# Modulation sums on VectorE and row tiles modulated piece by piece in a two-layer attention block on one Trainium2 core

## The reference

```python
def hybrid_layer(x, ctx, c, c_ctx, lw, pos, update_ctx):
    mod_x = jax.nn.silu(c) @ lw['ada_w'] + lw['ada_b']          # ada_w is 1024 x 3072
    mod_c = jax.nn.silu(c_ctx) @ lw['ada_w'] + lw['ada_b']
    shift, scale, gate = jnp.split(mod_x[:, None, :], 3, axis=-1)
    c_shift, c_scale, c_gate = jnp.split(mod_c, 3, axis=-1)
    h = rmsnorm(x, lw['norm_w']) * (1 + scale) + shift
    hc = rmsnorm(ctx, lw['norm_w']) * (1 + c_scale) + c_shift
    p = h @ lw['w_in']
...
    x = x + gate * merge_branches(o_m, o_s, o_a, z_m, z_s, z_a, g, lw)
    if update_ctx:                                               # layer 0 only
...
        ctx = ctx + c_gate * merge_branches(oc_m, oc_s, oc_a, zc_m, zc_s, zc_a, gc, lw)
    return x, ctx

def merge_branches(o_m, o_s, o_a, z_m, z_s, z_a, g, lw):
...
    y = jax.nn.sigmoid(g_m) * y_m + jax.nn.sigmoid(g_s) * y_s + jax.nn.sigmoid(g_a) * y_a
    return y @ lw['w_out']
```

## Time and profile before

| what | value |
|---|---|
| median of three runs | 2024.87 us (2021.86 to 2031.04) |
| profiled execution, its own time | 2025.76 us |
| its span | 2024.0 us |
| TensorE busy, share of the span | 89% |
| VectorE, ScalarE, GpSimd | 52%, 53%, 30% |
| layer 0's merge stage | 925.82 to 1100.52 us |
| layer 0's output projection | 1100.52 to 1177.94 us |
| layer 1's merge stage | 1869.32 to 1964.22 us |

### The profile page before, as it was taken

One profiled execution on the slowest core, in us unless ns is written; L12 is line 12 of the kernel. 1 busy time (PEld: TensorE's weight loads), 2 busy tenths in 40 slices (PEclk: granted clock), 3 DMA queues, 4 the chain that ended last, 5 costly groups with the idle time before them and its releaser, 6 DMA issues. The chain is left out here.

```text
span 2024.0 us, 27323 instructions
## 1 busy us (share of the span) xinstructions
PE 1794.5 (89%) x10749; PEld 1547.1 (76%) x10749; DVE 1048.1 (52%) x2082; ACT 1075.1 (53%) x1933; POOL 599.1 (30%) x328
## 2 busy tenths in 40 slices
PE   5597997999998999998888978887889988999887
PEld 2386887889997889897676966776878877887667
DVE  1524577666555465654323354376565555665323
ACT  1323677666666676664322243476666656775322
POOL 0332222212212222223545252322223232331651
PEclk9698999999999999999988989898999998999989
DMA  6220101011211111113433212101012221121542
GB/s 228 60 53 14 36 20 43 22 37 37 56 50 42 36 38 43 42 42 121 128 123 107 63 64 59 41 20 42 22 40 70 68 57 43 53 55 49 144 134 84
DMA packets 192286, 125.88 MB, mean 62 GB/s; under 512 B 21468, under 2 KB 187934, under 8 KB 192158
## 3 DMA queue, kind: packets, MB, share of 16 engines
q1 hardware_dynamic: 187248, 108.57, 19.0%
q10 hardware_dynamic: 3630, 11.37, 1.5%
q0 software_dynamic: 1280, 4.20, 0.6%
HBM read 119.92 MB, written 4.19 MB: 61 GB/s over the span
## 5 line engine op out<-in xcount | busy, mean ns | idle before, releaser
L1556 POOL TENSOR_TENSOR w_lo<-w_raw,w_hi 128x1024 fp32r<-128x1024 f32 (+3 forms) x220 | 462.7, 2111 | 1160.0 <-ACT w_hi L1373 1159.6
L1183 PE MATMUL acc<-h_hi,w_hi 128*128 128x512 f32 (+2 forms) x1288 | 474.1, 368 | 49.5 <-POOL w_lo L1556 27.0
L1183 PE MATMUL acc<-h_hi,w_lo 128*128 128x512 f32 (+2 forms) x1288 | 468.2, 363 | 0.0
L1183 PE MATMUL acc<-h_lo,w_hi 128*128 128x512 f32 (+2 forms) x1288 | 462.2, 361 | 0.0
L1183 PEld LDWEIGHTS acc<-h_hi,w_hi 128*128 128x128 f32 (+1 forms) x1288 | 249.7, 194 | 93.0 <-issue 25.4
L1469 ACT ACTIVATE pt<-ptp 128x512 fp32r<-128x512 f32 (+3 forms) x312 | 165.8, 563 | 269.8 <-PE ptp L1226 269.2
L1743 DVE TENSOR_REDUCE nmax<-wide 128x1 f32<-128x768 f32 (+3 forms) x240 | 189.9, 791 | 207.6 <-PE wide L1206 206.0
L1183 PEld LDWEIGHTS acc<-h_hi,w_lo 128*128 128x128 f32 (+1 forms) x1288 | 249.5, 194 | 36.9
L1183 PEld LDWEIGHTS acc<-h_lo,w_hi 128*128 128x128 f32 (+1 forms) x1288 | 247.4, 192 | 37.3
L1373 ACT ACTIVATE w_hi<-w_raw 128x1024 fp32r<-128x1024 f32 (+3 forms) x220 | 199.6, 921 | 76.1 <-DMA w_raw<-in_w_out 66.9
L1768 DVE TENSOR_TENSOR pt<-ptp,pt 128x512 fp32r<-128x512 f32 (+3 forms) x312 | 192.1, 641 | 53.8 <-ACT pt L1469 53.7
(11 more groups left out here) (193 smaller groups left out, 3299.6 us busy)
## 6 DMA issues: line engine op xcount, KB each, us to landing
w_raw<-in_w_in SPq DMA_DIRECT2D x102, 512.0 KB, 3.8
w_raw<-in_ada_w SPq DMA_DIRECT2D x48, 512.0 KB, 3.9
w_raw<-in_w_out SPq DMA_DIRECT2D x16, 512.0 KB, 3.8
xres<-in_x ACTq DMA_DIRECT2D x2, 2048.0 KB, 9.7
w_raw<-in_w_o_mla SPq DMA_DIRECT2D x16, 256.0 KB, 2.8
w_raw<-in_w_o_swa SPq DMA_DIRECT2D x16, 256.0 KB, 2.7
w_raw<-in_w_o_ax SPq DMA_DIRECT2D x16, 256.0 KB, 2.9
w_raw<-in_mla_w_uq SPq DMA_DIRECT2D x16, 144.0 KB, 2.3
```

Source lines behind the costliest of these rows:

```text
L1183: ins = nc.tensor.matmul(dst, lhs, rhs, start=first, stop=last)
L1556: nc.gpsimd.tensor_tensor(w_lo[s][:, 0:k], w_raw[s][:, 0:k], f(w_hi[s][:, 0:k]), ALU.subtract).then_inc(w_lo_ready, 1)
```

## The change

**Sums on VectorE.** `row_sums` replaces `ada` for layer 0's gate, layer 1's shift and scale, and layer 1's gate. A chunk (`adr`) is now 128 rows of `ada_w` by 1024 columns, loaded as it is into one of six half slots (`HALF`) or two side slots (`SIDE`), and never split. The event `AD` lets VectorE multiply chunk k by the k-th column of `cs_n` (one value a partition) and add it to a running sum in PSUM, `wide` for the latents and `ptp` for the context; the eighth result goes to SBUF. There are 32 such operations in layer 0's merge stage, 16 in its output projection, 8 in layer 1's merge stage, all of 128 x 1024. TensorE then only adds the partitions: `adg` multiplies ones by 512 columns of the sum (four groups in layer 0, two in layer 1), `adc` multiplies 128-column pieces of the sum by two columns of ones (16 products; once for shift, once for scale). Two or one broadcast DMAs put the bias into `gate` beforehand, and shift and scale find it in `vec`. In layer 0 three, three, two, three, three and two rows stand behind tiles 0 to 5; the gate sums stand behind tile 3, the shift sums behind tile 6. The scale rows stand behind every second group of the output projection. In layer 1 two rows stand behind each of tiles 0 to 3, the gate sums behind tile 4. Merge weights use four slots. The load of `xres` stands before tile 7 in layer 0 and before tile 5 in layer 1 instead of before tile 6.

**Row tiles.** `XM` is now eight operations of 128 x 128, each one multiplication and one addition, from PSUM to SBUF; ScalarE takes `h_hi` in two halves, the first after four of them.

The core of the diff:

```diff
+        due = (3, 3, 2, 3, 3, 2, 0, 0) if l + 1 < LAYERS else (2, 2, 2, 2, 0, 0, 0, 0)
+        sums_at = {3: gate_sums, 6: shift_sums} if l + 1 < LAYERS else {4: gate_sums}
         for t in range(KD):
-            if t == KD - 2:
-                usable[0] = ROOMY
+            if t == max(sums_at) + 1:
                 merge += step_of(load_rows(l))
...
             merge += y_tile(l, 2, t, og)
             if t == 0:
-                usable[0] = SLOTS
-            if t % 2 == 0:
-                merge += ada(l, GATES[t // 2])
-            if l + 1 < LAYERS:
-                merge += ada(l + 1, t)
+                usable[0] = ROOMY
+            if t in sums_at:
+                merge += sums_at[t]()
+            for row, k in rows_due[sum(due[:t]):sum(due[:t + 1])]:
+                merge += row(k)
...
+                if tt == x_first(l)[1] and j == 3 and side_row:
+                    run_all(side_sums())
                 g = go(group("wout", chunk_ids=cc, act=False, cost=cost_of(256, 3 * KD), mode="wout", l=l, j=j, tt=tt, xl=n["xl"],
                              gates=gates, needs=lambda: dict(l_done=y_ready)))
+                if sides and n["xr"] % 2 == 0:
+                    run_all(sides.pop(0))
...
+            elif mode == "adc":
+                for s in range(2):
+                    held_ = w_raw[slot_of[g["chunks"][s]]]
+                    for j in range(KD):
+                        at = 2 * (s * KD + j)
+                        run(a[:, at:at + 2], [(held_[:, j * P:(j + 1) * P], ones[:, 0:2])])
+            elif mode == "adg":
+                held_ = w_raw[slot_of[g["chunks"][g["side"]]]]
+                run(a[:, :], [(ones[:, :], held_[:, g["half"] * 512:(g["half"] + 1) * 512])])
...
-                    nc.scalar.activation(h_hi[:, :, tt * P:(tt + 1) * P], m, ACT.Copy).then_inc(x_h, 1)
+                    nc.scalar.activation(h_hi[:, 0:up, ts], m[:, 0:up, :], ACT.Copy)
+                    if new(x_f, i + 1):
+                        act.wait_ge(x_f, i + 1)
+                    nc.scalar.activation(h_hi[:, up:KD, ts], m[:, up:KD, :], ACT.Copy).then_inc(x_h, 1)
...
+                    for s in e["sides"]:
+                        total = (wide, ptp)[s][:, 0:D]
+                        column = cs_n[:, k, s:s + 1]
+                        if k == 0:
+                            ins = nc.vector.tensor_scalar(total, raw[:, :], column, None, ALU.mult)
+                        else:
+                            dst = total if k < KD - 1 else (w_raw[slot_of[e["left"]]] if s == 0 else raw)[:, :]
+                            ins = nc.vector.scalar_tensor_tensor(dst, raw[:, :], column, total, ALU.mult, ALU.add)
+                    ins.then_inc(ada_used, 1)
...
-                    nc.vector.tensor_tensor(m, w, mod_a[:, s, :].unsqueeze(2).to_broadcast([P, KD, P]), ALU.mult).then_inc(x_f, 1)
-                    if new(x_f, i + 1):
-                        dve.wait_ge(x_f, i + 1)
-                    nc.vector.tensor_tensor(m, m, mod_col[:, 0:KD, s].unsqueeze(2).to_broadcast([P, KD, P]), ALU.add).then_inc(x_b, 1)
+                    for k in range(KD):
+                        w = slice(k * P, (k + 1) * P)
+                        ins = nc.vector.tensor_scalar(x_mod[:, i % 2, w], xt_of(i)[:, w], mod_a[:, s, k:k + 1], mod_col[:, k, s:s + 1],
+                                                      ALU.mult, ALU.add)
+                        if k == KD // 2 - 1:
+                            ins.then_inc(x_b, 1)
+                    ins.then_inc(x_f, 1)
```

More of the change, by code:

```diff
@@ L161, in split_ahead @@
     def split_ahead():
+        while n["split"] < len(chunks) and n["split"] in whole:
+            n["split"] += 1
         c = n["split"]
@@ L166, in split_ahead @@
             return
-        if c <= last_used[0] + max(2, usable[0] - 2):
+        if c - sum(w in whole for w in range(last_used[0], c)) <= last_used[0] + max(2, usable[0] - 2):
             emit("W", c=c)
@@ L483, in ada, with row_sums, one, run @@
         return steps + [(read, 0)]
+    def row_sums(l, third, slots):
+        sides = (0, 1) if third < 2 or l + 1 < LAYERS else (0,)
+        cc = []
+        def one(k):
+            c = chunk("adr", l, third, k, sides, slot=slots[k % len(slots)])
+            whole.add(c)
+            cc.append(c)
+            def run():
+                n["ad"] += 1
+                used[c] = n["ad"] if k < KD - 2 else None
+                emit("AD", c=c, k=k, sides=sides, n=n["ad"], s=n["s"], left=cc[KD - 2] if k == KD - 1 else None)
+            return step_of(run)
+        def spread():
+            shape = dict(chunk_ids=(cc[KD - 2], cc[KD - 1]), act=False, l=l, third=third, needs=lambda: dict(used=n["ad"]))
+            if third == 2:
+                gs = [group("adg", mode="adg", cost=cost_of(4 * 512), side=s, half=half, bias=n["bias"] + len(sides), **shape)
+                      for s in sides for half in range(2)]
+                n["bias"] += len(sides)
+                return [st for g in gs for st in g["steps"]]
+            g = group("adc", mode="adc", cost=cost_of(256, 16), **shape)
+            def read():
+                if third == 1:
+                    emit("MOD", l=l, free=n["free"])
+                    n["mod"] += 1
+            return g["steps"] + [(read, 0)]
+        return one, spread
     def load_rows(l):
         def run():
-            emit("XL", l=l, tail=True, acc=n["acc"])
+            emit("XL", l=l, tail=True, acc=n["acc"], ad=n["ad"])
             n["xl"] += 1
         return run
-    COLUMNS, GATES = range(2 * D // 256), range(2 * D // 256, 3 * D // 256)
-    ada_made = []
+    COLUMNS = range(2 * D // 256)
+    ada_made, used = [], {}
     def z_tile(l, b, t, zs, og):
@@ L931, in chunk_dma @@
                         for i, c0 in enumerate((C_SV, C_AV))]
+            if kind == "adr":
+                third, k = chunks[c][2:4]
+                return [(raw, t_in["ada_w"][l, k * P:(k + 1) * P, third * D:(third + 1) * D])]
             if kind in ("ada", "wout"):
@@ L985, in _ @@
                     sp.dma_start(dst, src).then_inc(raw_load[slot_of[c]], 16)
+                if chunks[c][0] == "adr" and chunks[c][2:4] == (2, 0):
+                    l, sides = chunks[c][1], chunks[c][4]
+                    for s in sides:
+                        row = t_in["ada_b"][l:l + 1, 2 * D:3 * D]
+                        sp.dma_start(gate[:, s, :], row.to_broadcast([P, D])).then_inc(gate_load, 16)
                 if chunks[c][0] == "ada" and chunks[c][3] == 0:
@@ L1088, in matmuls @@
                             pairs += split3(hi[:, k, ts], lo[:, k, ts], w_hi[s][:, w], w_lo[s][:, w])
[L1089 removed]
+                    run(a[0:4 if mode == "adaF" else P, i * 256:(i + 1) * 256], pairs)
             elif mode == "vm":
@@ L1166, in _ @@
                                     pe.wait_ge(raw_load[slot_of[c]], loads[c])
-                        elif g["chunks"]:
+                        elif g["chunks"] and mode not in ("adc", "adg"):
                             if new(w_lo_ready, splits_to[g["chunks"][-1]]):
```

126 lines of the change are left out of this document (80 added, 46 removed).

## The result

The changed kernel takes 1948.01 us (median of four runs, 1945.92 to 1949.66) against 2027.95 for the kernel before in the same comparison: a ratio of 0.9607, 95% interval 0.9584 to 0.963. The forecast was 1942, between 1922 and 1972. The profiled execution took 1948.43, its span is 1946.6, 77.4 less than the span before.

A forecast was written before the change was run, and what follows sets the result against it. TensorE, busy 1794.5 of 2024.0 us, was taken as the bound. Terms of -59 and -19 (merges), +4.3 (scale), -6.5 (row tiles) and -4 (between layers) sum to -84, from 2025.76 to 1942 us, range 1922 to 1972.

The forecast's parts named there:

- main case: Whole kernel: all terms come about as summed, 1942 us, expected within 1925 to 1960; chance 0.75.
- Gate sums: Layer 0's merge: four groups of one 128x512 fp32 product by ones add 4.7 us on TensorE, up to 6.5.
- VectorE's pace: Layer 0's merge: VectorE, at 2.44 us a row, falls slightly behind the y tiles, costing 1 us (0 to 4).
- y_lo at the end: End of each merge: TensorE's next stage waits for the last tile's y_lo, 2.0 us in layer 0, 4.1 in layer 1.
- Start of the merge: First tile of each merge: tile 1's gate weights come late and hold ScalarE's th_x, 1.5 us, at worst 7 or 6.
- Shift sums: Layer 0's merge: 16 two-column fp32 products add 3.8 us on TensorE (3 to 4.5).
- the scale: Layer 0's output projection: row work hidden, 16 column-sum products and their reading add 4.3 us (+3 to +10).
- The row tiles: Prologue: one-pass modulation cuts the pitch from 4.6 to 3.7 us, first projection 6.5 us earlier (-9 to -2).
- Between the layers: Before layer 1's first product: faster tiles shorten the h_hi wait, low halves queue behind h_lo, net -4 us (-9 to +3).
- VectorE held by GpSimd: Merges and output projection: row operations slow to 2.5 us and VectorE becomes the bound, 1992 us; chance 0.08.
- Transfers late: Both merges: rows and weights arrive too slowly, +13 and +12.6 us, 1968 us together; chance 0.10.
- The clock: Both merges: new gaps in every tile drop TensorE to 1.2 GHz, kernel slower at 2085 us; chance 0.03.

The follow-up runs named there:

- weights-first run: Changed kernel with the second y tile's weights loaded ahead of the first rows in both merge stages: 1934.49 us, 1934.73 when run again.
- early split: Changed kernel with layer 1's first two weight chunks split ahead of the row tiles again, low halves before the four h_lo: 1951.06 us, ratio 0.9643.

## Why the prediction was right, and where it was not

- *Bound and main case.* TensorE's time and its waits in the merge stages were the place, and both stages came out as y tiles with little else. The sum of -84 was 6.6 too good. That it was no more is in part luck: the two merges came out 4.1 and 2.8 longer than their sums, and a wait of 2.35 that no term held went the other way (below).
- *Gate sums*, 4.7: the four products and the bank took 3.79 + 0.16. *VectorE's pace*, 1 of lag: none; a row operation is 1.28 us, not 1.22, but the tiles hold it. The bound of 13.5 us for a three-row tile was too high (11.15 measured), and with it the share of 77% for VectorE (60%): both took over the old busy time, with one-time work and with the context's y_lo at 2310 ns, which now takes 418. *y_lo at the end*, 2.0: 2.0; in layer 1, where I put 4.1, 3.2.
- *Start of the merge*, 1.5 in each stage: this is the step that failed most. In layer 0 the wait was 3.93, and the 12 products behind it took 5.46 instead of 2.96: 6.4, near the upper end that I had named. That is one execution; in the repeat of the changed kernel it was the wait of 2.5 alone, and over the six profiles with this order the wait lies between 2.4 and 4.0. I said that TensorE had a second bank to go on with; it does, and it ran through the context's gate products on it, but the third group needs the bank that th_x holds. In layer 1 it was the low half of tile 1's weights, 3.6, with 1.6 of slow clock. The place, ScalarE's order, was right, and the weights-first run took the waits away.
- *Shift sums*, 3.8: 3.63, but I had no term for the clock, which fell behind them in this execution and cost 1.65. The scale sums, 3.63 too, were followed by 48 products in 7.47, where 5.94 is seen at the full clock; that I put the scale at +4.3 and read +1.2 is because a wait for xn of 2.35 (before the transposes at 1171.55 in the kernel before) went at the same time, and TensorE's busy time there grew by 3.6.
- *The row tiles*, -6.5 and, in part, -4: shown to be worth 13 to 15 in all. Up to the first projection they bring 5.70, and the -4.4 of the table has a later start in it. A piece lasts 0.40 us, above the 0.2 to 0.3 that I gave as a sign, but the pieces came every 0.33 us (2.64 a tile), between my bounds, and ScalarE's pitch went to 3.45. What I missed is the stretch behind layer 1's first product, 3 to 4 us.
- *Between the layers*: the queue of low halves behind the four h_lo came as described, w_lo ending at 1131.23, but it cost more than I gave it: the wait grew from 6.42 to 8.17, where I had it shrink. The early split shows 3.40 with the queue gone.
- *The rivals.* VectorE held by GpSimd: no row operation has a tail (the 49 of L1885 take 1273 to 1290 ns), and the pieces read from PSUM none either while h_lo ran beside them. The rule of the Trainium skill ("SBUF — State Buffer", § Who interferes with whom) that a VectorE instruction with at most one SBUF input, outside the two-port modes, does not contend with GpSimd agrees with this: 402 ns median, 411 at most for 48 pieces. Its case of tensor_scalar on SBUF data, which it says can contend, was not seen held either: the first operations of the sums, which write to PSUM, take 1274 to 1282 ns, and GpSimd was busy with a w_lo beside the first two. Transfers late: only at the start, and through the order of two queues, not through their rate: once the second tile has begun, TensorE waits for no weights in either merge. The clock: lost for a few us behind the two starts and the column sums, never for a stage.
- *What no term held*: +3.3 and -4.0 us in stretches that the change does not touch. Their waits are the same before and after (50.3 and 50.3 us, 67.7 and 67.9), so it is TensorE's pace (granted clock 0.98 and 0.97, 0.95 and 0.96); two executions of the weights first differ by as much there (830.2 and 834.8, 646.4 and 652.8). That the two nearly cancel is luck.

## What to carry to other kernels

When a resource's queue gets new work in front of old, ask what it delays in each engine that takes from it in order: here five transfers ahead of one chunk held ScalarE, ScalarE held a bank, and TensorE stood for 2.4 to 4.0 us and in some executions lost up to 2.5 more to the clock, which making that chunk first gives back. Work moved to an idle engine is free until it fills the tile that hides it; the row of that tile (11.15 of 12.62 us busy) says how far it is from that. And a few us of gain are read from the stage that was edited, not from the whole, where untouched code differs by more from one execution to the next.

## What was not expected of the hardware

Behind 16 fp32 products of two columns each, which TensorE's rows show as 3.63 us without a gap, the granted clock was 0.68 for 5.4 us; with 32 columns a product they took 3.65 us and the clock behind them was 0.69. But in another execution the clock behind the same 16 products stayed at 1.00 for 5.4 us, and so it did in two executions behind the 16 of the scale sums, so these products alone do not decide it. Behind four fp32 products of 512 columns, 3.79 us, the next 24 products took 5.73, the full clock's time.
